# One PSUM bank and one masked copy for both directions of a scan level

## What is computed

```
def hgrn2_mixer(aq, ai, af_f, af_b, ag, lb_f, lb_b, g_norm, s0_f, s0_b):
    q = jax.nn.silu(split_heads(aq, A_HEADS))
    i = split_heads(ai, A_HEADS)
    ...
    o_f, s_f = hgrn2_chunk_scan(q, k_f, i, lf_f, s0_f)
    flip = lambda a: jnp.flip(a, axis=1)
    o_b, s_b = hgrn2_chunk_scan(flip(q), flip(k_b), flip(i), flip(lf_b), s0_b)
    o = o_f + flip(o_b)
    o = o * lax.rsqrt(jnp.mean(o * o, axis=-1, keepdims=True) + EPS)
```

## Time and profile before

| | us |
|---|---|
| median of 3 runs | 2515.48 |
| lowest, highest run | 2515.2, 2519.99 |
| the profiled execution, its own time | 2519.1 |
| its span in the trace | 2516.9 |
| PE busy | 2025.0 (80%) |
| DVE busy | 1757.2 (70%) |
| ACT busy | 976.9 (39%) |
| POOL busy | 945.0 (38%) |

### The profile page before, as it was taken

The page is one execution under the profiler, slowest core; times in us unless marked ns, Lnnn a source line. Parts: engine busy times, 40 slices in busy tenths (PEclk is TensorE's granted clock), DMA queues, the critical chain, the costliest instruction groups (busy, mean ns, idle before and its releaser), DMA issues. The chain is left out here.

```text
span 2516.9 us, 27358 instructions
## 1 busy us (share of the span) xinstructions
PE 2025.0 (80%) x6925; PEld 1124.5 (45%) x6925; DVE 1757.2 (70%) x3969; ACT 976.9 (39%) x2481; POOL 945.0 (38%) x774
## 2 busy tenths in 40 slices
PE   6978898956777689989698777787868788787876
PEld 2577845845665544477454222232223222232322
DVE  2732278888887867767787777777777777777774
ACT  1402144233445435312433443444444444344443
POOL 0020022223232312202233554565646565456654
PEclk9998999977777799989899998999999999999999
DMA  8844678853333379869698999999999999999997
GB/s 318 287 161 157 223 288 323 321 194 118 117 117 118 118 269 341 317 251 396 259 381 327 421 421 374 422 422 422 421 407 409 422 422 421 412 411 422 422 421 330
DMA packets 113299, 805.53 MB, mean 320 GB/s; under 512 B 12596, under 2 KB 14006, under 8 KB 17046
## 3 DMA queue, kind: packets, MB, share of 16 engines
q0 software_dynamic: 93760, 680.96, 67.8%
q1 hardware_dynamic: 17704, 118.17, 12.9%
q10 hardware_dynamic: 1712, 4.98, 0.5%
HBM read 800.79 MB, written 3.28 MB: 319 GB/s over the span
## 5 line engine op out<-in xcount | busy, mean ns | idle before, releaser
L1241 POOL DMA_INDIRECT RG<-in_uv,idxs x264 | 362.3, 1372 | 575.0 <-DVE PACC L1469 328.1
L982 ACT ACTIVATE agel<-apre 128x1 f32<-128x1 f32 x640 | 129.1, 202 | 939.0 <-DVE apre L1440 934.9
L624 PE MATMUL pl<-RG,BP 128*128 128x512 f32 x576 | 298.0, 643 | 104.8 <-ACT BP L998 103.6
L624 PE MATMUL pl<-RING,BP 128*128 128x512 f32 x576 | 280.7, 620 | 61.0 <-ACT BP L998 60.2
L1440 DVE CUSTOM_DVE_ANT_0 R<-RG,AB 128x1024 f32<-128x1024 f32 x201 | 246.8, 1230 | 101.9 <-DMA RG<-in_uv,idxs 83.2
L1241 POOL DMA_INDIRECT RING<-in_uv,idxs x168 | 241.8, 1439 | 160.7 <-PE pl L624 75.4
L1440 DVE CUSTOM_DVE_ANT_0 R<-RING,AB 128x1024 f32<-128x1024 f32 x168 | 205.9, 1226 | 96.1 <-DMA RING<-in_uv,idxs 79.1
L649 PE MATMUL pa<-HL,RING 128*128 128x512 f32 (+2 forms) x800 | 243.7, 462 | 1.8 <-issue 0.9
L624 PEld LDWEIGHTS pl<-RG,BP 128*128 128x128 f32 x576 | 101.0, 194 | 293.1 <-ACT BP L998 217.5
L998 ACT ACTIVATE BP<-CT,wexp 128x128 f32<-128x128 f32 x480 | 192.7, 401 | 54.5 <-PE pl L624 17.8
L624 PEld LDWEIGHTS pl<-RING,BP 128*128 128x128 f32 x576 | 104.4, 194 | 232.2 <-ACT BP L998 139.7
(11 more groups left out here) (322 smaller groups left out, 3369.6 us busy)
## 6 DMA issues: line engine op xcount, KB each, us to landing
RING<-in_in_slabs SPq DMA_DIRECT2D x42, 1024.0 KB, 5.8
RING<-in_pq_slabs SPq DMA_DIRECT2D x24, 1152.0 KB, 5.7
RING<-in_ada_slabs SPq DMA_DIRECT2D x16, 1024.0 KB, 5.1
RING<-in_out_slabs SPq DMA_DIRECT2D x12, 1024.0 KB, 6.2
RG<-in_col_slabs POOLq DMA_DIRECT2D x8, 1024.0 KB, 7.0
RING<-in_o_slabs SPq DMA_DIRECT2D x8, 1024.0 KB, 6.0
RG<-in_uv,idxs POOLq DMA_INDIRECT x297, 12.3
RING<-in_uv,idxs POOLq DMA_INDIRECT x168, 14.5
```

Source lines behind the costliest of these rows:

```text
L624: last = nc.tensor.matmul(acc[:, c * 512:(c + 1) * 512], DG[:, k % 2, :], bufs[k % len(bufs)][:, D + c * 512:D + (c + 1) * 512], start=Fal ...
L982: A(agel[:, par, k:k + 1], apre[:, par, k:k + 1], ACT.Gelu).then_inc(gel_done, 1)
L1241: nc.gpsimd.indirect_dma_start(out=bufs[b], out_offset=None, in_=uv, in_offset=bass.IndirectOffsetOnAxis(ap=idxs[:, par, k:k + 1], axis=0) ...
```

## The change

Both directions of a level go into one PSUM bank. The forward products cover only the columns of the odd blocks' queries, the backward ones only those of the even blocks; each product has 64 moving columns in place of 128. One mask holds both, and one copy takes the bank over. So a level is one name, with twice the weight in the planner's shares. DVE's updates must not overwrite the queries before the forward products have read them, and the bank's signal now comes only after the backward ones; a new semaphore `lvl_read` is raised after the forward products. The masks are 8 in place of 15.

```diff
@@ STAGES @@
-          ("merged", 40, {"diag": 1.0, "lvl": 1.0, "kT": 1.0, "dS": 1.0, "oA": 1.0, "qkT": 1.0, "sc": 1.0, "pT": 1.0,
+          ("merged", 40, {"diag": 1.0, "lvl": 2.0, "kT": 1.0, "dS": 1.0, "oA": 1.0, "qkT": 1.0, "sc": 1.0, "pT": 1.0,
@@ plan_groups @@
-            names.extend(("lvl", u, l, d) for d in range(2))
+            names.append(("lvl", u, l))
...
-        if nxt[0] == "lvl" and nxt[3] == 0:
+        if nxt[0] == "lvl":
@@ PE, levels @@
                 for l in range(LEVELS):
+                    ps = start(("lvl", u, l))
+
+                    def half(x, d):
+                        return x.rearrange("p (n a c) -> p n a c", a=2, c=1 << l)[:, :, 1 - d]
+
                     for d in range(2):
                         pe.wait_ge(hg_ready[d], (LEVELS + 1) * u + l + 1)
-                        ps = start(("lvl", u, l, d))
                         for b in range(4):
-                            last = mm(ps[:, bl[b]], HK[d][:, bl[b]], hq[d][:, bl[b]])
-                        finish(("lvl", u, l, d), last)
+                            last = mm(half(ps[:, bl[b]], d), HK[d][:, bl[b]], half(hq[d][:, bl[b]], d))
+                        if d == 0:
+                            last.then_inc(lvl_read, 1)
+                    finish(("lvl", u, l), last)
@@ ACT, tail @@
-                        beside.before(("lvl", v + 1, i + 1, 1))
+                        beside.before(("lvl", v + 1, i + 1))
@@ POOL, scan @@
-                    beside.before(("lvl", u, l, 1))
-                    wait_full(pool, ("lvl", u, l, 1))
+                    beside.before(("lvl", u, l))
+                    wait_full(pool, ("lvl", u, l))
@@ DVE, levels @@
-                take(("diag", u), 14)
+                take(("diag", u), LEVELS)
                 for l in range(LEVELS):
-                    group(("lvl", u, l, 0))
+                    beside.before(("lvl", u, l))
+                    dve.wait_ge(lvl_read, LEVELS * u + l + 1)
                     for ins in half_update(0, l, mul, u):
                         step(ins)
                     dve.sem_inc(hg_ready[0], 1)
-                    take(("lvl", u, l, 0), l)
-                    take(("lvl", u, l, 1), 7 + l)
+                    take(("lvl", u, l), l)
@@ masks @@
-        masks[:, l] = same & ((s >> l) % 2 == 0) & ((t >> l) % 2 == 1)
-        masks[:, 7 + l] = same & ((s >> l) % 2 == 1) & ((t >> l) % 2 == 0)
-    masks[:, 14] = s == t
+        masks[:, l] = same & ((s >> l) % 2 != (t >> l) % 2)
+    masks[:, LEVELS] = s == t
```

More of the change, by code:

```diff
@@ L307, in build @@
         CT = sb("CT", [P, P + 640 + NCAND])
-        MK = sb("MK", [P, 15, P], U8)
+        MK = sb("MK", [P, LEVELS + 1, P], U8)
         condT = sb("condT", [P, 2, KD])
@@ L329, in build @@
         SEL = AB[0:2, 512:768].rearrange("p (a b) -> p a b", a=2)
-        MK4 = view(AB, 4096, 15, P)
+        MK4 = view(AB, 4096, LEVELS + 1, P)
         CONDB, CJUNK = view(AB, 768, 2, D), AB[:, 2816:2816 + D]
@@ L447, in build @@
         hg_ready = [sem("hgf_ready"), sem("hgb_ready")]
+        lvl_read = sem("lvl_read")
         hs_ready, kT_ready, st_ready = sem("hs_ready"), sem("kT_ready"), sem("st_ready")
@@ L1893, in shape_constants @@
     consts = np.concatenate([ident, mbias, iota, lay(cos), lay(sin)], axis=1)
-    masks = np.zeros((P, 15, P), f)
+    masks = np.zeros((P, LEVELS + 1, P), f)
     s, t = i[:, None], i[None, :]
```

## The result

The changed kernel takes **2531.94 us** (median of 4 runs, 2531.6 to 2534.72) against 2516.08 of the kernel before on the same chip: a ratio of 1.0063, 95% interval 1.0050 to 1.0076. It is 16 us slower, where 26 us faster was forecast. The profiled run took 2531.6 us with a span of 2529.8, 12.9 more than the span of before. The lines have moved: the masked copy (`take`) is L1613 (L1606 before), the half update L1605 (L1598), Pool's products L1290, the dot product of an expert slot L1447, the copy of the last attention output L1704 (L1697), the products L650.

The account below looks back on a forecast made before the run. DVE was taken to bound the stretch of units 1 to 4; copies 24, Pool's order 6, unit 0 1, less new waits 5, gave 26 us off, from the 2515.5 us median to 2489.5 us (8 in 10: 2480 to 2504).

Follow-up runs that it names:

- kernel with 82: The changed kernel with 82 do-nothing instructions added to DVE's list ahead of the expert loop: 2509.51 us, 0.9952 of the kernel before.
- kernel with 81: The changed kernel with 81 do-nothing instructions added to DVE's list ahead of the expert loop: 2498.58 us, 0.9900 of the kernel before.
- before_order: The kernel before with only the 21 expert slots between a level's halves moved behind the whole level: 2516.73 us, 0.9998 of the kernel before.
- undo0_pad45: The changed kernel with two banks and full-width products again in unit 0, plus 45 do-nothing instructions in DVE's list: 2492.35 us, 0.9881 of the kernel before.
- before_narrow: The kernel before with only the level products made half-width, except unit 1's first four levels: 2525.0 us, 1.0020 of the kernel before.

## What to carry to other kernels

Count the instructions that an edit adds or removes ahead of each loop (tested here on DVE alone), and look at the loop's returns in the new trace ("issue" stands at the branch, more instruction packets) before the edit is judged: here 31 us of placement hid some 22 us of gain, and 60 to 81 empty instructions brought them back. And when a matmul is made narrower without being made shorter, look at the granted clock of the stages where PE does little else.

## What the runs showed of the hardware

- At a return to a DVE loop of 304 instructions DVE stands 4.6 to 9.5 us when the body touches four blocks of 128 instructions, and not at all when it touches three; the switch lies between two neighbouring places (tile 4: 324.3 and 335.7 us). With three such loops 19 places apart, the first start must lie in 0 to 42 of 128 for none to stand; the kernel before was at 33, after at 89. With four blocks touched five or six packets of 8 KB are fetched in a pass (kernel with 82, tile 4), with three none or one (kernel with 81).
- A tile whose DMA is full (share 1.00) doesn't absorb such a stand: a pass takes 84 to 85 us in place of 79.5, and a tile with two stands 9 to 12 us more.
- Sixteen records of 128x128 by 64 columns take 2.00 us at the high clock and 3.68 at the low one, no less than those by 128 columns: both follow each other at 0.112 and 0.213 us, in runs of single columns too. In unit 0 the same 136 records ran at a granted clock of 0.98 at full width in before, 0.89 at full width in before_order and undo0_pad45, 0.55 at half width in before_narrow, 0.50 in after; with the forward half alone at full width it was 0.55.
